# First weight units of the feed-forward layers and of the projection taken token chunk by token chunk

## The chip, the cores and the metric

One Trainium2 chip, one of its cores. The metric is device time in microseconds (us) from the first to the last instruction; lower is better. Engines: PE (TensorE, matrix multiplications), DVE (VectorE), ACT (ScalarE), POOL (GpSimd), SP (SyncE, here a queue that issues DMAs).

## The reference, cut to what matters

One inference step of a two-layer decoder with 1024 prompt tokens and 8 x 4 sample tokens, 1056 token columns in all. Every sub-layer first norms its input; the change sits in the first steps after three of these norms.

```python
h = rmsnorm(x, norm_g[i, 1]) * (1 + sc) + sh          # per token
x = x + gt * swiglu(h, ffn_w_in[i], ffn_w_out[i])     # both layers
def swiglu(h, w_in, w_out):
    g, u = jnp.split(h @ w_in, 2, axis=-1)
    return (jax.nn.silu(g) * u) @ w_out
p = h @ w_in          # layer 1: q, k, v and indexer columns, the projection
```

## The kernel before, in words

Activations lie transposed, features on the 128 partitions (8 feature tiles, KD), tokens along the free axis, in three token chunks of 352 columns (CH, NCH). fp32 products are made of split halves: a value is rounded to a high half (ACT) and the rest is its low half; a product is three matmuls, high-high, low-high and high-low. One result of 128 rows by 352 tokens is a **group** of 8 x 3 = 24 matmuls in one PSUM bank (a feed-forward output tile of the down pass has only 6).

Weights come in units of 1 MB (SP), rounded by ACT (`split_hi`, L623, L814) and their low half made by POOL (`split_lo`, L647, L846; semaphore `w_lo` counts finished units).

The phases run in this order: a front phase with the pooling mixer, feed-forward layer 0 (`ffn_phase`, about 218 to 1018 us of the trace), the projection (`projection_phase`, about 1018 to 1273 us), indexing and attention, the output projection, feed-forward layer 1 (from about 2184 us), the last norm.

**The norm** (`SplitNorm`) works chunk by chunk. ACT squares the 8 tiles of a chunk (L247), the squares are added (L256, L259: chunk 0 on DVE, chunks 1 and 2 on POOL), PE sums over partitions (`pe_sums`, L267), DVE scales (`variance`, L314), ACT takes the root (`act_std`, L281), DVE the reciprocal (`invert`, L319). Then each tile goes through DVE (g, L344), ACT (high half, L291), DVE (low half, L348); `lo_ready` counts finished tiles. Chunk 2 also has the 32 sample columns (`sample`, L326 to L330, and L354). The order of each engine is written out by hand in `act_all`, `dve_all`, `pool_all` and `pe_chunk`. POOL has: adds of chunk 1, split of unit 0, adds of chunk 2, split of unit 1. `pe_chunk(ch)` first makes the sum of chunk ch+1, then waits for the tiles of chunk ch.

**The feed-forward loop** has 11 iterations of three weight units: two hold gate and up columns (a = 0, 1), one the down columns. For each a and chunk PE makes a gate group and an up group; ACT takes silu of the gate (L630), DVE multiplies it with up and splits the product (L716, L718, L720); then the down pass (L696 to L698, 24 output tiles of 6 matmuls) and DVE's residual add (L80). PE has all three chunks of a = 0, then all three of a = 1, then the down pass, which waits for the third unit (L680). In iteration 0 the first pass meets the norm's chunks one by one.

**The projection** has 9 units with two output tiles each (the last has one): for each tile all three chunks. PE takes unit 0 tile by tile, so only one group of each chunk is there to be done while the next chunk is normed. ACT and DVE evict a group in halves (L839, L894), SP writes them out (L796, L797). POOL makes the low half of unit u, then loads 16 pages of indexer keys (`load_index_pages`, L743), and so on for units 2 to 8 (L852 to L854).

Of the kernel before, what the change touches and what calls it, by code (L numbers as in the profile page):

```python
# [16 lines left out]
F32 = mybir.dt.float32  # L17
# [194 lines left out]
class SplitNorm:  # L212
# [80 lines left out]
    def act_all(self, act, split_weights):  # L293
# [12 lines left out]
        split_weights(1)  # L306
        self.act_hi(act, 16, 24)

    def dve_all(self, dve):
# [25 lines left out]
        for ch in range(NCH):  # L335
# [14 lines left out]
            if ch < 2:  # L350
                variance(ch + 1)
                invert(ch + 1)
        dve.wait_ge(self.s_hi, 1)
        dve.tensor_tensor(self.hlo[:, :, SEQ:T], self.hs[:], self.hhi[:, :, SEQ:T].bitcast(F32), ALU.subtract).then_inc(self.s_lo, 1)  # L354
        dve.wait_ge(self.lo_ready, 3 * KD)
        dve.wait_ge(self.s_lo, 1)

    def pool_all(self, pool, split_weights):
        self.add_squares(pool, 1)
        split_weights(0)  # L360
        self.add_squares(pool, 2)
        split_weights(1)
# [212 lines left out]
def ffn_phase(nc, c, d, layer):  # L575
# [3 lines left out]
    with ExitStack() as ctx:  # L579
# [8 lines left out]
        sg, af = norm.sq, norm.g  # L588
        raw_ready = [sem("raw_ready0"), sem("raw_ready1")]
# [8 lines left out]
        def _(sp):  # L598
# [5 lines left out]
            with sp.Fori(0, N - 1) as i:  # L604
                for a in range(3):

                    sp.wait_ge(w_lo, i * 3 + (3, 2, 4)[a])
                    sp.dma_start(raw[:, a % 2, :], src[bass.ds(i * 3 + 3 + a, 1)].rearrange("a p n -> (a p) n")).then_inc(raw_ready[a % 2], 16)

# [4 lines left out]
        def _(act):  # L614
# [40 lines left out]
        def _(pe):  # L655
            norm.pe_sums(pe, 0)

            def iteration(i, first):
                for a in range(2):
                    pe.wait_ge(w_lo, 3 * i + (a + 1))  # L660
                    hi = whi[:, a, :].rearrange("p (k s m) -> p k s m", k=KD, s=2)
                    lo = wlo[:, a, :].rearrange("p (k s m) -> p k s m", k=KD, s=2)
                    for ch in range(NCH):
                        col = slice(ch * CH, (ch + 1) * CH)
                        if a == 0 and first:
                            norm.pe_chunk(pe, ch)
                        for side in range(2):
                            bank = 2 * ch + side
                            if a == 0 and not first:
                                pe.wait_ge(added, i * GD + (bank - 5))  # L670
# [4 lines left out]
                            for k in range(KD):  # L675
                                pe.matmul(c.ps[:, bank, 0:CH], hi[:, k, side, :], hhi[:, k, col], start=(k == 0), stop=False)  # L676
                                pe.matmul(c.ps[:, bank, 0:CH], lo[:, k, side, :], hhi[:, k, col], start=False, stop=False)  # L677
                                last = pe.matmul(c.ps[:, bank, 0:CH], hi[:, k, side, :], hlo[:, k, col], start=False, stop=(k == KD - 1))  # L678
                            last.then_inc(up_ready if side else gate_ready, 1)
# [3 lines left out]
                for ch in range(NCH):  # L683
                    col = slice(ch * CH, (ch + 1) * CH)
                    pe.wait_ge(a_ready, i * 6 + (NCH + ch + 1))
# [19 lines left out]
        def _(dve):  # L705
            norm.dve_all(dve)

            with dve.Fori(0, N) as i:
                for a in range(2):
                    for ch in range(NCH):  # L710
                        q = a * NCH + ch
                        dve.wait_ge(silu_ready, i * 6 + (q + 1))
                        dve.wait_ge(up_ready, i * 6 + (q + 1))
                        s = af[:, q % 2, :]
                        col = slice(ch * CH, (ch + 1) * CH)
                        dve.tensor_tensor(s, sg[:, q % 2, :], c.ps[:, 2 * ch + 1, 0:CH], ALU.mult).then_inc(gated, 1)  # L716
                        dve.wait_ge(gated, i * 6 + (q + 1))
                        dve.tensor_copy(ahi[:, a, col], s).then_inc(a_step, 1)  # L718
                        dve.wait_ge(a_step, i * 6 + (q + 1))
                        dve.tensor_tensor(alo[:, a, col], s, ahi[:, a, col].bitcast(F32), ALU.subtract).then_inc(a_ready, 1)  # L720
                        if q >= 1:
                            dve.wait_ge(a_ready, i * 6 + q)
                for ch in range(NCH):
                    for m in range(KD):
# [4 lines left out]
                        residual_add(dve, c, c.ps[:, q % 6, 0:CH], m, ch, 2 * layer + 1, tmp[:], (rstep, i * KD + (m + 1)), added)  # L729
            dve.wait_ge(added, N * GD)  # L730
# [16 lines left out]
def projection_phase(nc, c, d):  # L747

    NU = 9
    with ExitStack() as ctx:  # L750
# [24 lines left out]
        n_split = [m for m in MS if split_tile(m) is not None]  # L775
        n_f32 = [m for m in MS if f32_dst(m) is not None]
# [3 lines left out]
        def _(sp):  # L780
# [4 lines left out]
            for m in MS:  # L785
                u = m // 2
                if m % 2 == 0 and u + 2 < NU:
                    sp.wait_ge(w_lo, u + 1)
                    sp.dma_start(raw[:, u % 2, :], d.win[u + 2]).then_inc(raw_ready[u % 2], 16)
                for ch in range(NCH):  # L790
                    col = slice(ch * CH, (ch + 1) * CH)
                    sp.wait_ge(act_read, 3 * m + ch + 1)
                    if split_tile(m) is not None:
                        sp.wait_ge(dve_read, 3 * m + ch + 1)
                        q = (3 * n_split.index(m) + ch) % 3
                        sp.dma_start(d.halves[split_tile(m), 0, :, col], shi[:, q, :].bitcast(F32)).then_inc(split_out[q], 16)  # L796
                        sp.dma_start(d.halves[split_tile(m), 1, :, col], slo[:, q, :].bitcast(F32)).then_inc(split_out[q], 16)  # L797
                    if f32_dst(m) is not None:
                        q = (3 * n_f32.index(m) + ch) % 3
                        sp.dma_start(f32_dst(m)[:, col], sf[:, q, :]).then_inc(f32_out[q], 16)  # L800
# [3 lines left out]
            for q in range(3):  # L804
                sp.wait_ge(split_out[q], 32 * len(n_split))
                sp.wait_ge(f32_out[q], 16 * len(n_f32))

        @block.scalar
        def _(act):
            def split_hi(u):  # L810
                act.wait_ge(raw_ready[u % 2], 16 * (u // 2 + 1))
                if u >= 2:
                    act.wait_ge(ready, 6 * (u - 1))
                act.activation(whi[:, u % 2, :], raw[:, u % 2, :], ACT.Copy).then_inc(w_hi, 1)  # L814
            norm.act_all(act, split_hi)
            n = 0
            for m in MS:
                if m % 2 == 0 and m >= 2 and m // 2 + 1 < NU:
                    split_hi(m // 2 + 1)
                for ch in range(NCH):  # L820
                    act.wait_ge(ready, 3 * m + ch + 1)
                    src = c.ps[:, (3 * m + ch) % 6, 0:CH]
                    last = None
                    if f32_dst(m) is not None:
                        k = n_f32.index(m)
                        if k:
                            act.wait_ge(f32_out[ch], 16 * k)
                        last = act.activation(sf[:, ch, :], src, ACT.Copy)
                    if m in samples and ch == 2:
                        last = act.activation(sq[:, samples.index(m), :], src[:, CP2:CH], ACT.Copy)  # L830
                    if split_tile(m) is not None:
                        k = n_split.index(m)
                        if k:
                            act.wait_ge(split_out[ch], 32 * k)
                        if last is not None:
                            last.then_inc(step, 1)
                            n += 1
                            act.wait_ge(step, n)
                        last = act.activation(shi[:, ch, :], src, ACT.Copy)  # L839
                    last.then_inc(act_read, 1)  # L840
# [17 lines left out]
        def _(pe):  # L858
            norm.pe_sums(pe, 0)

            def unit(u, slot, first=False, tiles=2):
                pe.wait_ge(w_lo, u + 1)
                hi = whi[:, slot, :].rearrange("p (k m) -> p k m", k=KD)
                lo = wlo[:, slot, :].rearrange("p (k m) -> p k m", k=KD)
                for m in range(tiles):
                    for ch in range(NCH):
                        q = 3 * m + ch
                        if first and m == 0:
                            norm.pe_chunk(pe, ch)
                        if not first:  # L870
                            pe.wait_ge(act_read, u * 6 + (q - 5))
                            pe.wait_ge(dve_read, u * 6 + (q - 5))
                        col = slice(ch * CH, (ch + 1) * CH)
                        for k in range(KD):
                            w = slice(m * P, (m + 1) * P)
                            pe.matmul(c.ps[:, q, 0:CH], hi[:, k, w], hhi[:, k, col], start=(k == 0), stop=False)  # L876
                            pe.matmul(c.ps[:, q, 0:CH], lo[:, k, w], hhi[:, k, col], start=False, stop=False)
                            last = pe.matmul(c.ps[:, q, 0:CH], hi[:, k, w], hlo[:, k, col], start=False, stop=(k == KD - 1))
# [1033 lines left out]
```

## Time and profile before

| what | value |
|---|---|
| three runs | 3021.97, 3023.41, 3024.28 us; median 3023.41 |
| profiled execution | span 3025.1 us, and no time outside it is shown |
| PE busy | 2520.1 us, 83% of the span |
| DVE, POOL, ACT busy | 48%, 25%, 23% |
| mean granted clock of PE | 0.911 of full speed |

PE is the engine with the most work, so time is won where PE stands still or runs at the lower clock. In the timeline a line has the start in us, the duration in us, the engine, the program line, the operation, what it writes and reads, and in brackets how long its engine was idle before it and what ended that.

### The profile page before, as it was taken

How to read it: one execution, taken by the hardware profiler on the slowest of the kernel's cores; microseconds unless marked ns; L12 is line 12 of the kernel's file. 1: busy time of each engine (PE TensorE's matmuls, PEld its weight loads, DVE VectorE, ACT ScalarE, POOL GpSimd, SP SyncE). 2: the span in 40 equal slices, each digit the busy share in tenths (PEclk: the TensorE clock that was granted, in tenths of full speed). 3: DMA queues.
4: the chain of work that ended last, by engine and by line, in shares of the span. 5: the costliest groups of instructions: out<-in, count | busy, mean ns of one | idle time of the engine just before them, and what ended most of it. 6: DMA issues, size and time to landing. Idle time of an engine off the chain costs nothing. (4 is left out here: it accounts for less than half of the span.)

```text
span 3025.1 us, 40642 instructions
## 1 busy us (share of the span) xinstructions
PE 2520.1 (83%) x14573; PEld 2225.2 (74%) x14573; DVE 1439.8 (48%) x3100; ACT 694.4 (23%) x1162; POOL 744.9 (25%) x557
## 2 busy tenths in 40 slices
PE   7866999999999689784312789697869999999995
PEld 3446999999999589741112567345869999999994
DVE  2747333333333730179997578344273333333336
ACT  2113111111110322150001888312131111111101
POOL 0223121121121235410000677521131211221110
PEclk9887999999999799896655999888979999999997
DMA  9421111111110234552121110571011111111101
GB/s 368 166 94 56 42 42 42 42 42 69 42 42 14 99 113 162 152 121 81 56 69 28 39 32 16 182 268 56 29 56 42 42 42 42 42 64 47 42 14 57
DMA packets 89864, 230.67 MB, mean 76 GB/s; under 512 B 15764, under 2 KB 52724, under 8 KB 73396
## 3 DMA queue, kind: packets, MB, share of 16 engines
q1 hardware_dynamic: 75856, 205.33, 19.6%
q0 software_dynamic: 10400, 22.18, 2.3%
q10 hardware_dynamic: 3524, 2.07, 0.2%
q8 instruction: 49, 0.80, 0.1%
q14 instruction: 35, 0.29, 0.0%
HBM read 200.77 MB, written 28.76 MB: 76 GB/s over the span
## 5 line engine op out<-in xcount | busy, mean ns | idle before, releaser
L676 PE MATMUL ps<-f_hhi,f_whi 128*128 128x352 f32 x2112 | 687.2, 325 | 33.9 <-DVE f_hlo L348 18.4
L677 PE MATMUL ps<-f_hhi,f_wlo 128*128 128x352 f32 x2112 | 681.7, 323 | 0.0
L678 PE MATMUL ps<-f_hlo,f_whi 128*128 128x352 f32 x2112 | 680.9, 322 | 0.0
L647 POOL TENSOR_TENSOR f_wlo<-f_raw,f_whi 128x2048 fp32r<-128x2048 f32 x66 | 304.0, 4607 | 1110.1 <-ACT f_whi L623 1110.1
L80 DVE SCALAR_TENSOR_TENSOR xT<-ps,mod,xT 128x352 f32<-128x352 f32 (+1 forms) x576 | 327.9, 572 | 219.8 <-PE ps L698 121.4
L676 PEld LDWEIGHTS ps<-f_hhi,f_whi 128*128 128x128 f32 x2112 | 400.4, 190 | 37.6 <-DVE f_hlo L348 37.6
L677 PEld LDWEIGHTS ps<-f_hhi,f_wlo 128*128 128x128 f32 x2112 | 401.0, 190 | 0.0
L678 PEld LDWEIGHTS ps<-f_hlo,f_whi 128*128 128x128 f32 x2112 | 400.1, 189 | 0.0
L696 PE MATMUL ps<-f_ahi,f_whi 128*128 128x352 f32 x1056 | 340.6, 323 | 0.0
L697 PE MATMUL ps<-f_ahi,f_wlo 128*128 128x352 f32 x1056 | 338.3, 320 | 0.0
L698 PE MATMUL ps<-f_alo,f_whi 128*128 128x352 f32 x1056 | 338.1, 320 | 0.0
L623 ACT ACTIVATE f_whi<-f_raw 128x2048 fp32r<-128x2048 f32 x66 | 126.4, 1915 | 554.2 <-PE ps L698 418.2
L1396 POOL TENSOR_TENSOR pa_pr<-pa_pr,pa_rl 128x128 f32<-128x128 f32 (+7 forms) x128 | 142.8, 1147 | 368.1 <-DVE pa_rl L1376 368.0
L716 DVE TENSOR_TENSOR f1n_g<-f1n_sq,ps 128x352 f32<-128x352 f32 x66 | 34.4, 521 | 399.4 <-PE ps L678 396.9
L716 DVE TENSOR_TENSOR f0n_g<-f0n_sq,ps 128x352 f32<-128x352 f32 x66 | 34.4, 521 | 398.1 <-PE ps L678 395.7
L697 PEld LDWEIGHTS ps<-f_ahi,f_wlo 128*128 128x128 f32 x1056 | 198.4, 188 | 0.0
L696 PEld LDWEIGHTS ps<-f_ahi,f_whi 128*128 128x128 f32 x1056 | 198.1, 188 | 0.0
L698 PEld LDWEIGHTS ps<-f_alo,f_whi 128*128 128x128 f32 x1056 | 197.9, 187 | 0.0
L876 PE MATMUL ps<-pj_hhi,pj_whi 128*128 128x352 f32 x408 | 135.0, 331 | 19.0 <-DVE pj_hlo L354 11.0
L1067 PE MATMUL ps<-ix_part,rowsum 128*128 128x1 f32 x64 | 16.3, 324 | 156.3 <-DVE ix_rel L1165 156.2
L179 PE MATMUL ps<-ada_raw,silu 128*9 128x256 f32 x576 | 129.2, 388 | 14.5 <-ACT silu L431 14.5
L1316 PE MATMUL ps<-kst,pa_qst 128*128 128x512 f32 (+3 forms) x192 | 75.2, 392 | 73.7 <-DMA pa_qst<-halves 41.7
(307 smaller groups left out, 3939.0 us busy)
## 6 DMA issues: line engine op xcount, KB each, us to landing
f_raw<-in_ffn SPq DMA_DIRECT2D x66, 1024.0 KB, 4.8
ada_raw<-in_ada SPq DMA_DIRECT2D x36, 1024.0 KB, 5.0
sa_kv<-in_ckv POOLq DMA_DIRECT2D x54, 256.0 KB, 4.3
ix_vT<-in_ada SPq DMA_DIRECT2D x12, 1024.0 KB, 4.8
sa_kv<-in_ckv SPq DMA_DIRECT2D x42, 256.0 KB, 4.4
pj_raw<-in_win SPq DMA_DIRECT2D x9, 1024.0 KB, 5.8
pa_qst<-halves SPq DMA_DIRECT2D x128, 64.0 KB, 2.4
halves<-pj_shi SPq DMA_DIRECT2D x45, 176.0 KB, 1.9
```

The costliest lines, as they stand in the source:

```text
L80: ins = dve.scalar_tensor_tensor(out=x, in0=psum[:, 0:n], scalar=gate[:, 0:1], in1=x, op0=ALU.mult, op1=ALU.add)
L179: last = pe.matmul(self.sums(u), self.c.silu[:, k, :], w[:, k, :], start=(k == 0), stop=(k == KD - 1))
L623: act.activation(whi[:, a, :], raw[:, a % 2, :], ACT.Copy).then_inc(w_hi, 1)
L647: pool.tensor_tensor(wlo[:, a, :], raw[:, a % 2, :], whi[:, a, :].bitcast(F32), ALU.subtract).then_inc(w_lo, 1)
L676: pe.matmul(c.ps[:, bank, 0:CH], hi[:, k, side, :], hhi[:, k, col], start=(k == 0), stop=False)
L677: pe.matmul(c.ps[:, bank, 0:CH], lo[:, k, side, :], hhi[:, k, col], start=False, stop=False)
L678: last = pe.matmul(c.ps[:, bank, 0:CH], hi[:, k, side, :], hlo[:, k, col], start=False, stop=(k == KD - 1))
L696: pe.matmul(c.ps[:, q % 6, 0:CH], hi[:, k, w], ahi[:, k, col], start=(k == 0), stop=False)
L697: pe.matmul(c.ps[:, q % 6, 0:CH], lo[:, k, w], ahi[:, k, col], start=False, stop=False)
L698: last = pe.matmul(c.ps[:, q % 6, 0:CH], hi[:, k, w], alo[:, k, col], start=False, stop=(k == 1))
L876: pe.matmul(c.ps[:, q, 0:CH], hi[:, k, w], hhi[:, k, col], start=(k == 0), stop=False)
L1396: pool.tensor_tensor(p, p, rl[:, i % 3, g:g + 1].to_broadcast([P, (q + 1) * P]), ALU.mult).then_inc(p_ready, 1)
```

## The change

In iteration 0 of each feed-forward layer PE takes, for each chunk, the gate and up groups of a = 0 and of a = 1 (four groups) before the next chunk. q = 2 ch + a numbers these pairs. In the projection it takes, for each chunk, the four tiles of units 0 and 1. The second unit is therefore split earlier: on ACT right behind chunk 0's high halves, on POOL ahead of chunk 2's adds. The evictions (silu and gates; high and low halves) of chunk 0 are put on ACT and DVE ahead of chunk 2's norm (`between(0)`), the rest behind the norm (`between(1)`). Iteration 0 is taken out of ACT's and DVE's loops. Core of the diff:

```diff
     def act_all(self, act, split_weights, between):
...
         split_weights(0)
         self.act_hi(act, 0, 8)
+        split_weights(1)
         self.act_std(act, 1)
...
         self.act_std(act, 2)
-        split_weights(1)
+        between(0)
         self.act_hi(act, 16, 24)
+        between(1)
     def dve_all(self, dve, between):
...
             if ch < 2:
                 variance(ch + 1)
                 invert(ch + 1)
+            if ch == 1:
+                between(0)
...
         dve.wait_ge(self.s_lo, 1)
+        between(1)
     def pool_all(self, pool, split_weights):
         self.add_squares(pool, 1)
         split_weights(0)
+        split_weights(1)
         self.add_squares(pool, 2)
-        split_weights(1)
 # ffn_phase
+        FIRST = [(0, 1), (2, 3, 4, 5)]
+            def first_silus(qs):
+                for q in qs:
+                    act.wait_ge(gate_ready, q + 1)
+                    if q >= 2:
+                        act.wait_ge(gated, q - 1)
+                    act.activation(sg_first(q), c.ps[:, 2 * (q % 3), 0:CH], ACT.Silu).then_inc(silu_ready, 1)
-            norm.act_all(act, lambda a: split_hi(a, 0, True))
+            norm.act_all(act, lambda a: split_hi(a, 0, True), lambda half: first_silus(FIRST[half]))
             split_hi(2, 0, True)
-            with act.Fori(0, N - 1) as i:
+            for a in range(3):
+                split_hi(a, 1)
+            with act.Fori(1, N - 1) as i:
+            def first_up():
+                for ch in range(NCH):
+                    norm.pe_chunk(pe, ch)
+                    for a in range(2):
+                        q = 2 * ch + a
+                        if ch == 0:
+                            pe.wait_ge(w_lo, a + 1)
+                        for side in range(2):
+                            if q >= 3:
+                                pe.wait_ge(gated if side else silu_ready, q - 2)
+                            group(a, side, 2 * (q % 3) + side, ch)
+            norm.dve_all(dve, lambda half: first_gates(FIRST[half]))
+            down(0)
+            with dve.Fori(1, N) as i:
 # projection_phase
+        ORDER = [(m, ch) for ch in range(NCH) for m in range(4)] + [(m, ch) for m in range(4, 17) for ch in range(NCH)]
             def split_hi(u):
                 act.wait_ge(raw_ready[u % 2], 16 * (u // 2 + 1))
                 if u >= 2:
-                    act.wait_ge(ready, 6 * (u - 1))
+                    act.wait_ge(ready, 10 if u == 2 else 6 * (u - 1))
+            def evict(n):
+                m, ch = ORDER[n]
+                act.wait_ge(ready, n + 1)
...
+                    if k >= 3:
+                        act.wait_ge(split_out[k % 3], 32 * (k // 3))
...
+            def first_evictions(half):
+                for n in range(0, 4) if half == 0 else range(4, 12):
+                    evict(n)
+            norm.act_all(act, split_hi, first_evictions)
+            for n in range(12, len(ORDER)):
+                m, ch = ORDER[n]
+                if ch == 0 and m % 2 == 0:
+                    if m == 4:
+                        split_hi(2)
+                    if m // 2 + 1 < NU:
+                        split_hi(m // 2 + 1)
+                evict(n)
+            def first_units():
+                for ch in range(NCH):
+                    norm.pe_chunk(pe, ch)
+                    for m in range(4):
+                        n = 4 * ch + m
+                        if ch == 0 and m % 2 == 0:
+                            pe.wait_ge(w_lo, m // 2 + 1)
+                        if n >= 6:
+                            pe.wait_ge(act_read, n - 5)
+                            pe.wait_ge(dve_read, n - 5)
+                        group(m // 2, m % 2, n % 6, ch)
```

DVE's `gate(...)` holds the three instructions of L716 to L720, with a wait for its own last one in q = 0 and 1; `first_gates(qs)` calls it. DVE's `first_low(half)` makes the low halves of groups 0 to 3 and 4 to 11. SP walks ORDER too, and asks for units 2 and 3 at n = 0 and n = 1.

## Rows read from the trace of the kernel before

**Rows 1.** Waits of PE over the span: total us, times, longest us.

```profile
PE ps L676 <- DVE f_hlo L348: 18.4, 4, 5.4
...
PE ps L676 <- DVE f_hlo L354: 15.5, 2, 7.9
```

**Rows 2.** Engines in layer 0's first gate and up passes; PEclk is third from the end.

```profile
242.50:307.40 64.90, 52.87 (x291) 51.77 (x292) 39.90 (x55) 23.02 (x37) 20.90 (x10) 0.88 0.14 50
```

**Rows 3.** Timeline of PE in layer 0: start, duration, operation, idle before.

```profile
242.54 0.66 PE L676 MATMUL ps<-f_hhi,f_whi 128*128 128x352 f32 x1 [5.42 <-DVE f_hlo L348]
...
252.84 0.86 PE L267 MATMUL ps<-f0n_rstd,ones 128*128 128x352 f32 x2
258.06 0.66 PE L676 MATMUL ps<-f_hhi,f_whi 128*128 128x352 f32 x1 [4.36 <-DVE f_hlo L348]
...
275.16 0.63 PE L676 MATMUL ps<-f_hhi,f_whi 128*128 128x352 f32 x1 [7.62 <-DVE f_hlo L354]
...
307.38 0.32 PE L696 MATMUL ps<-f_ahi,f_whi 128*128 128x352 f32 x1
```

**Rows 4.** Timeline of DVE in layer 0: reciprocal, low half, sample columns, gates.

```profile
243.48 2.35 DVE L319 RECIPROCAL f0n_rstd<-f0n_rstd 128x352 f32<-128x352 f32 x1 [0.56 <-ACT f0n_rstd L281]
...
248.31 1.30 DVE L348 SCALAR_TENSOR_TENSOR f_hlo<-f0n_g,mod,f_hhi 128x352 fp32r<-128x352 f32 x1
...
261.39 4.34 DVE L326 TENSOR_TENSOR f0n_hs<-xT,f0n_rstd 128x256 f32<-128x256 f32 x1
...
300.03 0.52 DVE L716 TENSOR_TENSOR f0n_g<-f0n_sq,ps 128x352 f32<-128x352 f32 x1 [6.17 <-PE ps L678]
...
300.96 0.53 DVE L720 TENSOR_TENSOR f_alo<-f0n_g,f_ahi 128x352 fp32r<-128x352 f32 x1
307.65 0.52 DVE L716 TENSOR_TENSOR f0n_g<-f0n_sq,ps 128x352 f32<-128x352 f32 x1 [6.17 <-PE ps L678]
```

**Rows 5.** Timeline of POOL in layer 0: four adds of chunk 2, split of unit 1.

```profile
248.28 4.50 POOL L259 TENSOR_TENSOR f0n_rstd<-f0n_rstd,f0n_sq 128x352 f32<-128x352 f32 x4 [0.29 <-ACT f0n_sq L247]
260.85 4.61 POOL L647 TENSOR_TENSOR f_wlo<-f_raw,f_whi 128x2048 fp32r<-128x2048 f32 x1 [8.06 <-ACT f_whi L623]
```

**Rows 6.** Timeline of ACT in layer 0: weight split, table load, a silu.

```profile
258.88 1.89 ACT L623 ACTIVATE f_whi<-f_raw 128x2048 fp32r<-128x2048 f32 x1
...
275.71 1.28 ACT L630 ACT_TABLE_LOAD   x1
...
288.49 0.47 ACT L630 ACTIVATE f0n_sq<-ps 128x352 f32<-128x352 f32 x1 [1.11 <-PE ps L678]
```

**Rows 7.** Timeline of PE in layer 1 and in the projection.

```profile
2209.22 0.66 PE L676 MATMUL ps<-f_hhi,f_whi 128*128 128x352 f32 x1 [5.42 <-DVE f_hlo L348]
...
2275.33 0.32 PE L696 MATMUL ps<-f_ahi,f_whi 128*128 128x352 f32 x1
...
1043.83 0.66 PE L876 MATMUL ps<-pj_hhi,pj_whi 128*128 128x352 f32 x1 [5.42 <-DVE pj_hlo L348]
...
1076.29 0.63 PE L876 MATMUL ps<-pj_hhi,pj_whi 128*128 128x352 f32 x1 [10.97 <-DVE pj_hlo L354]
```

**Rows 8.** DMA issues of the page: KB each, median us from issue to landing.

```profile
xT<-in_ckidx POOLq DMA_DIRECT2D x128, 32.0 KB, 2.1
...
halves<-pj_slo SPq DMA_DIRECT2D x45, 176.0 KB, 2.4
```

**Rows 9.** Timeline of POOL in the projection: splits of units 2 and 8, last page load.

```profile
1096.58 4.60 POOL L846 TENSOR_TENSOR pj_wlo<-pj_raw,pj_whi 128x2048 fp32r<-128x2048 f32 x1 [30.01 <-ACT pj_whi L814]
...
1236.80 4.62 POOL L846 TENSOR_TENSOR pj_wlo<-pj_raw,pj_whi 128x2048 fp32r<-128x2048 f32 x1
...
1259.29 0.52 POOL L743 DMA_DIRECT2D xT<-in_ckidx  x1 [0.77 <-issue]
```

**Rows 10.** End of the projection: eviction of the last group, next phase's first DMA.

```profile
1265.56 0.46 ACT L828 ACTIVATE pj_sf<-ps 128x352 f32<-128x352 f32 x1 [2.80 <-PE ps L878]
...
1273.04 0.38 SPq L947 DMA_DIRECT2D ix_vT<-o_vT  x1
```

More of the change, by code:

```diff
@@ L588, in ffn_phase @@
         sg, af = norm.sq, norm.g
+        sg0, af0 = sb("sg0", [P, 2, CH]), sb("af0", [P, CH])
         raw_ready = [sem("raw_ready0"), sem("raw_ready1")]
@@ L674, in iteration @@
                                 pe.wait_ge(gated, i * 6 + (ch + 1))
[L675 to L679, printed above, removed]
+                            group(a, side, bank, ch)
                 pe.wait_ge(w_lo, 3 * i + 3)
@@ L705, in _, with gate, down @@
         def _(dve):
[L706 to L722, printed above, removed]
+            def gate(i, q, s, sgq, bank, a, ch, alone=False):
+                dve.wait_ge(silu_ready, i * 6 + (q + 1))
+                dve.wait_ge(up_ready, i * 6 + (q + 1))
+                col = slice(ch * CH, (ch + 1) * CH)
+                dve.tensor_tensor(s, sgq, c.ps[:, bank, 0:CH], ALU.mult).then_inc(gated, 1)
+                dve.wait_ge(gated, i * 6 + (q + 1))
+                dve.tensor_copy(ahi[:, a, col], s).then_inc(a_step, 1)
+                dve.wait_ge(a_step, i * 6 + (q + 1))
+                dve.tensor_tensor(alo[:, a, col], s, ahi[:, a, col].bitcast(F32), ALU.subtract).then_inc(a_ready, 1)
+                if q >= 1:
+                    dve.wait_ge(a_ready, i * 6 + q)
+                if alone:
+                    dve.wait_ge(a_ready, q + 1)
+            def down(i):
                 for ch in range(NCH):
@@ L859, in _, with group, unit @@
             norm.pe_sums(pe, 0)
-            def unit(u, slot, first=False, tiles=2):
-                pe.wait_ge(w_lo, u + 1)
+            def group(slot, m, bank, ch):
                 hi = whi[:, slot, :].rearrange("p (k m) -> p k m", k=KD)
                 lo = wlo[:, slot, :].rearrange("p (k m) -> p k m", k=KD)
+                col = slice(ch * CH, (ch + 1) * CH)
+                for k in range(KD):
+                    w = slice(m * P, (m + 1) * P)
+                    pe.matmul(c.ps[:, bank, 0:CH], hi[:, k, w], hhi[:, k, col], start=(k == 0), stop=False)
+                    pe.matmul(c.ps[:, bank, 0:CH], lo[:, k, w], hhi[:, k, col], start=False, stop=False)
+                    last = pe.matmul(c.ps[:, bank, 0:CH], hi[:, k, w], hlo[:, k, col], start=False, stop=(k == KD - 1))
+                last.then_inc(ready, 1)
+            def first_units():
+                for ch in range(NCH):
+                    norm.pe_chunk(pe, ch)
[7 more added lines that the diff above has]
+                        group(m // 2, m % 2, n % 6, ch)
+            def unit(u, slot, tiles=2):
+                pe.wait_ge(w_lo, u + 1)
                 for m in range(tiles):
@@ L867, in unit @@
                         q = 3 * m + ch
[L868 to L878, printed above, removed]
-                        last.then_inc(ready, 1)
-            unit(0, 0, True)
-            unit(1, 1)
+                        pe.wait_ge(act_read, u * 6 + (q - 5))
+                        pe.wait_ge(dve_read, u * 6 + (q - 5))
+                        group(slot, m, q, ch)
+            first_units()
             with pe.Fori(1, 4) as i:
```

143 lines of the change are left out of this document (78 added, 65 removed).

## The prediction

> **What bounds the kernel now.** I read the waits of PE first, then the stretch of a first iteration, then the timelines of each engine there. In the waits [rows 1] the reader is to see that PE, the busiest engine, stands still for the norm: it waits for the low halves of a chunk (four times over both layers) and for the sample columns (twice). The stretch [rows 2] is layer 0 from its first gate matmul to its down pass: 64.9 us of which PE is busy 52.9, at a mean granted clock of 0.88. The timeline [rows 3] shows where: chunk 0 starts at 242.54, chunk 1 at 258.06 (4.36 us idle, and the 0.86 us sum just before), chunk 2 at 275.16 (7.62 us idle), the down pass at 307.38. After each wait the first matmul takes 0.63 to 0.66 us instead of 0.32: PE is back at the lower of its two levels, 1.2 GHz. Two figures follow. Warm, 48 matmuls take 7.63 us (gates at 300.03 and 307.65 [rows 4]), 0.159 us each. Chunk 0's pair took 252.84 - 242.54 - 0.16 = 10.14 us, so a cold start costs 2.5 us.
>
> **The work of PE is only moved.** No matmul is added or removed. Before, eight groups of 24 are left when chunk 2 is ready; afterwards four. That is the gain, 4 x 3.82 = 15.3 us, if chunk 2 is not later and nothing new waits. Both happen, so I follow the chains in layer 0.
>
> **Chunk 1.** ACT now splits unit 1 right after chunk 0's high halves, which end about 1 us before PE starts, at 241.6 (an estimate). So 1.89 us [rows 6] until 243.5, then POOL 4.6 us [rows 5] until 248.2. ACT's root of chunk 1 stands behind the split and comes 0.5 us later; the reciprocal, 2.35 us even while POOL adds [rows 4], ends at 246.3. Then DVE needs two SBUF operands, and such an instruction does not run while POOL splits: the sample product took 4.34 us [rows 4] because the split of unit 1 ran from 260.85 to 265.46 [rows 5]. So DVE stands until 248.2. POOL's seven adds of chunk 2 start only then, and ACT's square 19, which needs the first add, holds up the high halves queued behind it until 249.6; DVE's first three tiles cover that. While POOL adds, a DVE low half takes 1.30 us [rows 4] beside adds of 1.13 us [rows 5]. All seven adds now fall on DVE work, where before some fell on the reciprocal. Walked tile by tile with these prices, chunk 1 is ready at 260.8, 2.7 us later than before.
>
> Meanwhile PE has 96 matmuls of chunk 0: 242.54 + 10.14 + 7.63 = 260.3, the second unit being there since 248.2. Then comes the sum of chunk 2, 0.86 us, until 261.2. The late chunk is covered by 0.4 us; without cover, each us late counts. PE does chunk 1's 96 matmuls warm until 276.5.
>
> **Chunk 2.** Its scaling on DVE waits for that sum, which now stands behind chunk 0's four groups. From the sum it takes as long to the end of the reciprocal as from chunk 1's end to the sample product, 258.06 to 261.39, about 3.5 with the hop from PE: 264.7. ACT loads the silu table (1.28) and makes two silus (0.47 each) [rows 6] beside that reciprocal; even a load back would lie in ACT's wait for the sample columns. Then the two gates put ahead of the sample columns cost DVE 2 x (300.96 + 0.53 - 300.03 = 1.46) = 2.9 [rows 4]: 267.7. From the sample product's start to PE's chunk 2 it was 261.39 to 275.16, 13.8 us, of which the split took 4.34 less some 0.4 (estimate, from 0.53 for 352 columns). That split is gone from here: 9.85 us remain, chunk 2 at 277.6. PE idles 1.1 us. For the clock no row shows a wait this short here; bounds are 0 and 2.5, and I take 0. PE's four groups end at 277.6 + 15.25 = 292.85.
>
> **A new wait: the third unit.** ACT's split of the down weights now stands behind silu q = 5, which needs the last gate group at 277.6 + 11.45 = 289.05. Then 0.47 + 1.89 + 4.6 and the hops: 296.1. Before, it was ready long ahead. PE idles 3.2 us and starts cold (2.5; bounds 0 and 2.5; I take 2.5, as the 4.36 us wait is nearest). The down pass counts from 298.6 instead of 307.38: **8.8 us won**. DVE's last gate conversion is held up by the same split; its operands are needed only in the down pass's last third. SP's next load also waits for the third unit, 16 us later than before, but PE wants it 24 x 6 x 0.159 = 22.9 us after the down pass starts, and behind the two splits (6.5 us) 16 us are left for the load. So no loss.
>
> Layer 1 shows the same steps shifted by 2209.22 - 242.54 = 1966.7 [rows 7]: down pass at 2265.3 instead of 2275.33, **10.0 us**.
>
> **The projection**, shifted by 801.3 [rows 7]: sum of chunk 2 done at 1062.5, reciprocal 1066.0. Ahead of the sample columns stand four low halves; the fourth eviction reuses slot 0 and so waits until SP has written group 0 out: 0.53 for its low half, SP's two issues 0.4, 2.4 us to landing [rows 8], then 0.46 + 0.53. That ends at 1070.5 where low halves alone would end at 1068; chunk 2 at 1080.3 against 1076.29. SP asks for unit 3's megabyte ahead of group 1's output, but that slot is needed only at 1079. PE has idled 2.5 us; cold, its four groups end at 1098.1. Now the last eviction (0.7), ACT's split of unit 2, which stands behind it (1.89), and POOL's (4.6): PE waits 7.3 us, until 1105.4, and starts cold. POOL's split of unit 2 starts at 1100.8 instead of 1096.58 [rows 9], 4.2 later. From there POOL is the bound: splits and page loads run back to back, 140.2 us from the split of unit 2 to that of unit 8 [rows 9], while PE needs 6 x 22.9 = 137.3. So the low half of unit 8 is ready at 1245.6, PE ends at 1257.1 instead of 1265.5, the last page load lands at 1259.29 + 4.2 + 2.1 = 1265.6 [rows 8, 9]. Before, the next phase began 7.5 us after PE's end [rows 10]; from PE that would be 1264.6, so POOL's loads decide: about 1266 against 1273.04, **7.0 us**.
>
> **Sum.** 8.8 + 10.0 + 7.0 = 25.8 us. On the profiled execution's 3025.1 that is 2999.3; this execution is 1.7 us above the median of 3023.4, so the forecast is 2997.6. Its own range: with no cold starts behind the new waits 7.5 more (2990); with cold starts at chunk 2 in both layers and a landing 3 us later, 8 less (3005.6).
>
> **Rivals.** (a) Nothing new waits. Then the layers win 307.38 - 292.85 = 14.5 each, and the projection's PE runs on from 1098.1 over 39 groups of 3.815 to 1246.9, 18.6 us earlier: 2975.8. Against it stand ACT's order and POOL's back-to-back chain.
>
> (b) DVE and POOL share nothing in chunk 1. Then an add and a low half take turns, 1.13 + 0.57 = 1.7 us instead of 1.3, seven times: chunk 1 is 2.8 later, 2.4 of it uncovered, 7 us in three places: 3004.8. If the split holds the reciprocal up too, it is 2.35 more each: 3011.9. For it speaks the 4.34 us stall, against it the 1.30 us row and the reciprocal's 2.35. The Trainium skill, page SBUF — State Buffer, section Who interferes with whom, says that of a VectorE instruction with two SBUF inputs and a GpSimd one that reads SBUF the later is blocked until the first has finished; by that rule the first time of (b) would come out, while the row shows partial overlap, and the measurement decides.
>
> (c) The change does not do what it says: unit 1's low half comes no earlier than its 265.5. PE then waits 12.6 us inside chunk 0 and nearly all of the gain is gone: about 3020. Against it: only ACT's place in the order held that split back.
>
> (d) Slower. The new wait of 3.2 us before the down pass leaves PE at the lower level through the whole pass: 144 x 0.159 = 22.9 us per layer, and the 7.3 us wait does so to unit 2, 22.9 again: 68.7 less the 25.8: 3066. It turns the sign once 25.8 / 0.159 = 162 matmuls more run at half speed. Against it: 48 matmuls behind a 5.42 us wait lost only 2.5 us.
>
> **How the numbers follow.** The forecast 0.75, (a) 0.06, (b) 0.12, (c) 0.04, (d) 0.03. The range reaches from 2988 to 3008: it takes in the forecast's bounds and the first half of (b), and leaves out (a), (c), (d), the end of (b) and tails. Within 0.2% (6 us, about what a measurement of this kernel can tell from no change) lie (c) and a bit of (b): 0.05. Slower: 0.03. Faster: 0.92.
>
> **What would show it.** Right: no PE idle between chunk 0 and chunk 1, about 1 us ahead of chunk 2 in the layers and 2.5 in the projection, 3 us of idle put down to POOL's split ahead of the first down matmul, 7 us ahead of unit 2, and the next phase after the projection waiting for page loads. Wrong: an idle time ahead of chunk 1 (b), PE at the lower level long into the down pass (d), or no idle ahead of it (a).

## The result and the profile after

The changed kernel takes 3010.57 us (median of four runs, 3007.39 to 3013.15) against 3023.85 for the kernel before; the ratio is 0.9948, with an interval of 0.9934 to 0.9961. That is 11.8 to 20.0 us faster, where 25.8 were forecast. The profiled execution is the fastest of the four, 3007.39 us; its span is 3005.6.

What answers to [rows 1], the waits of PE (total us, times, longest), in the kernel after:

```profile
PE ps L1121 <- DMA ix_kiwi<-kiwi: 26.7, 1, 26.7
PE ps L686 <- DVE f_hlo L350: 21.7, 4, 10.2
...
PE ps L927 <- DVE pj_hlo L350: 12.3, 2, 10.2
```

The two entries of [rows 1] (18.4 and 15.5 us, six waits) have become one of 21.7 us in four waits. Two of these are the wait of 10.2 us ahead of chunk 0; the waits ahead of chunk 1 are gone. (The wait ahead of chunk 0 was 5.42 us before, because PE made the sum of chunk 1 later then, behind unit 0's low half; from the layer's first square to its first gate matmul it is 24.6 us in both kernels.) The new first line belongs to the phase behind the projection, and is the clue to what follows. Before, it was:

```profile
PE ps L1044 <- DMA ix_kiwi<-kiwi: 14.8, 1, 14.8
```

The stretch that answers to [rows 2], from layer 0's first gate matmul to its down pass, after (us, busy time of PE, PEld, DVE, ACT, POOL, then the granted clock third from the end):

```profile
243.96:297.50 53.54, 49.67 (x290) 48.56 (x290) 39.65 (x57) 19.74 (x36) 16.58 (x9) 0.95 0.00 1
```

64.9 us have become 53.5, and PE's clock there is 0.95 instead of 0.88. The timeline of PE after (start, duration, operation, idle before), in the order of layer 0, the projection, layer 1, answers to [rows 3, 7]:

```profile
243.96 0.66 PE L686 MATMUL ps<-f_hhi,f_whi 128*128 128x352 f32 x1 [10.16 <-DVE f_hlo L350]
278.88 0.40 PE L686 MATMUL ps<-f_hhi,f_whi 128*128 128x352 f32 x1 [0.65 <-DVE f_hlo L350]
297.54 0.66 PE L734 MATMUL ps<-f_ahi,f_whi 128*128 128x352 f32 x1 [3.16 <-POOL f_wlo L670]
298.00 0.49 PE L735 MATMUL ps<-f_ahi,f_wlo 128*128 128x352 f32 x1
...
1035.72 0.66 PE L927 MATMUL ps<-pj_hhi,pj_whi 128*128 128x352 f32 x1 [10.16 <-DVE pj_hlo L350]
1072.14 0.40 PE L927 MATMUL ps<-pj_hhi,pj_whi 128*128 128x352 f32 x1 [2.14 <-DVE pj_hlo L350]
1095.23 0.63 PE L927 MATMUL ps<-pj_hhi,pj_whi 128*128 128x352 f32 x1 [7.50 <-POOL pj_wlo L906]
...
2199.98 0.66 PE L686 MATMUL ps<-f_hhi,f_whi 128*128 128x352 f32 x1 [10.15 <-DVE f_hlo L350]
2234.82 0.40 PE L686 MATMUL ps<-f_hhi,f_whi 128*128 128x352 f32 x1 [0.70 <-DVE f_hlo L350]
2253.50 0.66 PE L734 MATMUL ps<-f_ahi,f_whi 128*128 128x352 f32 x1 [3.16 <-POOL f_wlo L670]
```

Every wait that the prediction placed is there, nearly in the size it gave. Yet the sum is missed. To see where, I cut both executions at the same events. A layer runs from chunk 0's first gate matmul to the first square of the next norm; the projection from its first square to the next phase's first DMA. Layers begin at 242.54 and 2209.22 [rows 3, 7] before, at 243.96 and 2199.98 after. For the kernel before, the first squares of the norms behind the layers lie at 1018.64 and 2986.58, for the kernel after at 1010.54 and 2966.84; the next phase's first DMA lies at 1273.04 [rows 10] and 1266.34:

| stage, us | before | after | won | forecast |
|---|---|---|---|---|
| layer 0 | 776.1 | 766.6 | 9.5 | 8.8 |
| layer 1 | 777.4 | 766.9 | 10.5 | 10.0 |
| projection | 254.4 | 255.8 | -1.4 | 7.0 |

The rest of the 19.5 us between the spans is 0.9 us in phases with the same code. So the layers gave what was forecast and the projection gave nothing, although PE ends earlier in it. The three stages give 18.6 us, which lies within the interval of the ratio. POOL, ACT and SP in the projection after, answering to [rows 9, 10]:

```profile
1090.49 4.50 POOL L906 TENSOR_TENSOR pj_wlo<-pj_raw,pj_whi 128x2048 fp32r<-128x2048 f32 x1 [40.91 <-ACT pj_whi L863]
...
1230.48 4.63 POOL L906 TENSOR_TENSOR pj_wlo<-pj_raw,pj_whi 128x2048 fp32r<-128x2048 f32 x1
...
1246.93 0.46 ACT L875 ACTIVATE pj_sf<-ps 128x352 f32<-128x352 f32 x1 [2.80 <-PE ps L929]
...
1253.55 0.52 POOL L792 DMA_DIRECT2D xT<-in_ckidx  x1 [0.85 <-issue]
...
1266.34 0.38 SPq L1024 DMA_DIRECT2D ix_vT<-o_vT  x1
```

PE's last group is evicted 236.4 us after the phase's first square, against 246.9 before [rows 10]; SP's next DMA, 7.5 us behind it before, now comes 19.4 us behind it. What ended the projection? In the profile each engine's part of a phase, its block, ends with an instruction called DRAIN, and the EVENT_SEMAPHOREs of all engines come together behind the last of these. The projection's last ones in the kernel before (engine's queue, operation, duration in ns, first and last start in us):

```profile
L750 POOLq DRAIN  x1: 9283/9283/9283, 1261.5 to 1261.5; - x1
...
L750 SPq DRAIN  x1: 7/7/7, 1271.7 to 1271.7; - x1
```

And in the kernel after:

```profile
L799 SPq DRAIN  x1: 7/7/7, 1253.4 to 1253.4; - x1
...
L799 POOLq DRAIN  x1: 9283/9283/9283, 1255.7 to 1255.7; - x1
L799 SPq EVENT_SEMAPHORE  x1: 17/17/17, 1265.1 to 1265.1; - x1
```

POOL ends its block with a DRAIN of 9.28 us. Before, it lay from 1261.5 to 1270.8, and SP, which waits for its last write, was done at 1271.7: the DRAIN was covered by 0.9 us and no wait pointed to it. After, SP is done at 1253.4 and then stands still until 1265.1. Measured from the phase's first square, SP's end moved from 253.1 to 242.9, but POOL's from 252.1 to 254.4, and the later of the two counts. PE's first work of the next phase waits 26.7 us instead of 14.8 for a transfer that SP can't issue sooner. POOL is later since its chain starts later: the split of unit 2 comes 79.95 us after the first square instead of 77.94, and to the split of unit 8 it is 139.99 us, against 140.22 before [rows 9]: the chain is back to back in both kernels.

### The profile page after: what moved, and what is told of

It is laid out like the page before. It is cut to its first block and busy times, and to the rows that moved or that the text cites. A ratio compares the mean times of both kernels' runs of the same rounds, so it can differ in the third digit from the quotient of the medians.

```text
span 3005.6 us, 40525 instructions
## 1 busy us (share of the span) xinstructions
PE 2511.4 (84%) x14573; PEld 2217.1 (74%) x14573; DVE 1435.8 (48%) x3100; ACT 670.1 (22%) x1144; POOL 744.0 (25%) x557
## 5 line engine op out<-in xcount | busy, mean ns | idle before, releaser
L686 PE MATMUL ps<-f_hhi,f_whi 128*128 128x352 f32 x2112 | 683.9, 324 | 21.9 <-DVE f_hlo L350 21.7
L927 PE MATMUL ps<-pj_hhi,pj_whi 128*128 128x352 f32 x408 | 134.1, 329 | 20.1 <-DVE pj_hlo L350 12.3
L1393 PE MATMUL ps<-kst,pa_qst 128*128 128x512 f32 (+3 forms) x192 | 75.2, 391 | 73.9 <-DMA pa_qst<-halves 41.6
```

Of the source, the lines that this page charges most:

```text
L927: pe.matmul(c.ps[:, bank, 0:CH], hi[:, k, w], hhi[:, k, col], start=(k == 0), stop=False)
```

## Experiments

The theory: POOL's chain of splits, page loads and DRAIN sets the projection's end. Rivals: PE's waits and clock, SP's writes, or a gain that is there and lost elsewhere. The ratios below are to the kernel before, of 4 to 11 executions each, and their intervals reach some 3 to 5 us to either side; the stages of the profiled executions are the finer measure. In stages whose code is the changed kernel's they spread from 765.3 to 768.2 us (layers) and from 255.0 to 257.7 us (projection).

| kernel | won, us (ratio, interval) | layer 0 | layer 1 | projection |
|---|---|---|---|---|
| layers only | 19.1 (0.9937, 0.9923 to 0.9950) | 767.8 | 765.3 | 255.0 |
| projection only | -1.8 (1.0006, 0.9997 to 1.0015) | 776.1 | 776.6 | 257.4 |
| pages ahead | 29.1 (0.9904, 0.9889 to 0.9919) | 768.1 | 768.2 | 248.3 |
| unit 2 early | 23.9 (0.9921, 0.9907 to 0.9936) | 766.3 | 765.7 | 249.3 |
| half of the loads | one execution, no ratio | 766.3 | 765.6 | 245.6 |
| down unit early | 18.5 (0.9939, 0.9926 to 0.9953) | 766.6 | 767.2 | 255.0 |
| three edits | 23.9 (0.9921, 0.9907 to 0.9934) | 766.7 | 767.2 | 249.3 |
| half a group ahead | 33.9 (0.9888, 0.9870 to 0.9906) | 766.4 | 767.5 | 238.9 |
| down unit early, wait | 28.4 (0.9906, 0.9891 to 0.9920) | 762.1 | 762.8 | 257.7 |
| half a group, wait | 43.6 (0.9856, 0.9841 to 0.9871) | 761.5 | 762.4 | 238.8 |

**Layers only.** The projection goes back to its old order, with the old norm class:

```diff
 # projection_phase
-        norm = SplitNorm(nc, ctx, "pjn", c, 2, hhi, hlo)
+        norm = SplitNormBefore(nc, ctx, "pjn", c, 2, hhi, hlo)
```

> The two feed-forward layers as changed, the projection as it was before. Theory (the end of the projection is set by POOL: its last page load, then a DRAIN of 9.28 us, so that the gain of PE there is lost): the layers' gains as read from the two traces remain, 9.6 + 10.6 = 20.2 us, and the 1.4 us that the projection's phase grew by are not paid. Faster than before by about 20 us, faster than the changed kernel by about 1.4 us, and the projection's phase, from its first square to the next phase's first DMA, takes 254.4 us again. Rival (the layers won less than the traces of single executions say, and the projection did win its 7.0): faster than before by only 8 to 13 us, slower than the changed kernel by 7.

Measured: 19.1 us faster than before, the projection 255.0 us. The layers alone give the whole gain.

**Projection only.** The other half:

```diff
 # ffn_phase
-        norm = SplitNorm(nc, ctx, f"f{layer}n", c, 2 * layer + 1, hhi, hlo)
+        norm = SplitNormBefore(nc, ctx, f"f{layer}n", c, 2 * layer + 1, hhi, hlo)
```

> The projection as changed, the two layers as they were before. Theory (POOL's last load and its DRAIN of 9.28 us set the end): no gain, 0 to 1.5 us slower than before; PE's last group is evicted some 20 us before the next phase's first DMA, POOL's DRAIN begins about 245 us after the phase's first square, and SP waits about 12 us at the block's end. Rival (my prediction's step: the end is the landing of the last load, and what was lost went elsewhere in the program): faster than before by 7 us.

Measured: 1.8 us slower, with an interval that reaches from 0.9 faster to 4.5 slower; 7 us faster lies well outside it. SP was done at 1263.9, POOL's DRAIN of 9283 ns began at 1266.1, which is 246.7 us after the first square. The two halves add up: 19.1 - 1.8 = 17.3 against 15.7 for both.

**Pages ahead.** A group of 16 loads goes ahead of the split of unit 2:

```diff
 # projection_phase, gpsimd
+            load_index_pages(pool, c, d, 0, page_ready)
             for u in range(2, NU):
                 split_lo(u)
-                load_index_pages(pool, c, d, u - 2, page_ready)
+                if u < NU - 1:
+                    load_index_pages(pool, c, d, u - 1, page_ready)
```

> The changed kernel, with POOL's first 16 page loads moved ahead of its split of unit 2 (the stretch in which POOL waits for that unit), so that nothing but the DRAIN follows its split of unit 8. PE's work and all waits of PE stay. Theory (POOL's chain with the DRAIN sets the end): POOL's DRAIN ends near 1245 us on the changed kernel's scale instead of 1265.0, then SP's last landing at 1253.4 decides, and the next phase begins near 1254.7 instead of 1266.3: 11.6 us less than the changed kernel, about 25 to 27 less than before. First rival (PE's chain sets the end: cold starts and the 7.5 us wait for unit 2): 0 us against the changed kernel. Second rival (the end is the last landing, not the DRAIN): a DRAIN of 9.28 us that now ends behind SP changes nothing by itself, and the gain is only that of the landing, 1255.7 - 1253.4 = 2.3 us.

Measured: a phase of 248.3 us, 7.5 less than after. The block's end in this kernel:

```profile
L799 POOLq DRAIN  x1: 12293/12293/12293, 1236.2 to 1236.2; - x1
...
L799 SPq DRAIN  x1: 7/7/7, 1257.3 to 1257.3; - x1
```

And POOL's last load and last split there:

```profile
1233.98 0.52 POOL L792 DMA_DIRECT2D xT<-in_ckidx  x1 [0.77 <-issue]
1234.51 4.63 POOL L906 TENSOR_TENSOR pj_wlo<-pj_raw,pj_whi 128x2048 fp32r<-128x2048 f32 x1
```

POOL is done at 1236.2 + 12.3 = 1248.5, and now SP's 1257.3 decides, as the theory said. The DRAIN is longer since it began while the last split ran (1234.51 to 1239.14); from that split's end it is 9.32 us, though the last load had been issued 5.2 us before that end and had landed. So the DRAIN does not wait for a recent load to land. Only 7.5 of 11.6 us came because the 16 loads did not fit in ahead of the split: it began 84.7 us after the first square, 4.8 later than after, PE waited 12.6 us for unit 2, and SP's end came 4.1 us later than after. PE's idle time grew and the phase got shorter, which rules out the rival of PE's waits; the second rival's 2.3 us are too little.

**Unit 2 early.** ACT makes unit 2's high half before the last two evictions:

```diff
 # projection_phase, first_evictions
                     evict(n)
+                    if n == 9:
+                        split_hi(2)
...
-                    if m == 4:
-                        split_hi(2)
```

> The changed kernel, with ACT's high half of unit 2 placed right behind the eviction of the tenth group instead of behind the twelfth (its condition, that PE is done with unit 0, is met there). Theory (POOL's back-to-back chain from the split of unit 2 sets the end): POOL's split of unit 2, the page loads and the DRAIN all come about 7.6 us earlier, PE's wait of 7.5 us ahead of unit 2 is gone, and the next phase begins about 7.6 us earlier: 7 to 8 us less than the changed kernel. Rival (the end of the phase depends on neither POOL nor PE, but on SP's queue of writes): under 1 us.

Measured: a phase of 249.3 us, 6.5 less than after; POOL's split of unit 2 came at 73.9 us instead of 79.95, and PE's wait of 7.5 us is gone. The DRAIN began at 1247.7, SP was done at 1245.5: POOL still ends last, by 2.2 + 9.3 us. Together with the kernel above this leaves POOL's chain alone as the bound: there PE waited longer and POOL ended earlier, here both came earlier, and each time the phase followed the later of POOL and SP.

**Half of the loads.** This kernel leaves out half of the page loads behind each split. `load_index_pages` gets two more arguments for it, how many pages of a group it loads and how many it skips:

```diff
 # projection_phase, gpsimd
-                load_index_pages(pool, c, d, u - 2, page_ready)
+                load_index_pages(pool, c, d, u - 2, page_ready, PAGES // 4)
...
```

> The changed kernel with 8 instead of 16 page loads behind each of POOL's splits in the projection (half of the indexer keys are not loaded, so their scores are left to what lies in the buffer). Theory (the length of POOL's DRAIN grows with the loads that POOL issued in the block: 9.28 us for 113, 2.38 us for 17 and 5.65 us for 63 in other blocks): a DRAIN of 4.6 to 5.3 us for 57 loads. Rival (a fixed length at this place): 9.28 us again. As POOL then has some 9 us of slack in each unit, the splits no longer run back to back, PE and SP's last landing set the end, and the phase is about 12 us shorter than the changed kernel's 255.8 us.

Its block's end:

```profile
L799 POOLq DRAIN  x1: 4710/4710/4710, 1226.3 to 1226.3; - x1
L799 SPq DRAIN  x1: 7/7/7, 1250.5 to 1250.5; - x1
```

57 DMAs of POOL in the block, 4.71 us; 113, 9.28 us. The difference is 4.573 us for 56 loads, 82 ns each. The phase is 10.2 us shorter (12 expected), and SP's last landing sets its end, 19.4 us behind POOL's.

**Down unit early.** This goes at the two waits of 3.16 us in the layers:

```diff
 # ffn_phase, scalar
             def first_silus(qs):
+                if qs[0] == 2:
+                    split_hi(2, 0, True)
                 for q in qs:
...
-            split_hi(2, 0, True)
```

> The changed kernel, with ACT's high half of the down unit placed ahead of the silus of q = 2 to 5 in the layers' first iteration instead of behind them. Theory (in both layers the down pass waits 3.16 us for POOL's low half of that unit, and then starts at the lower level for about 9 matmuls, some 1.3 us): both go, 4.5 us per layer, about 9 us less than the changed kernel; the down pass begins without an idle time put down to POOL's split. Rival (the 1.89 us that ACT then spends ahead of the silus delays the gate groups that need them, and gives the gain back): 0 to 3 us less than the changed kernel, with a new wait of PE for ACT's silu.

Measured: nothing, 766.6 and 767.2 us; but neither theory nor rival is what the trace shows. PE, DVE and POOL in layer 0:

```profile
292.01 9.23 POOL L671 TENSOR_TENSOR f_wlo<-f_raw,f_whi 128x2048 fp32r<-128x2048 f32 x2 [8.79 <-ACT f_whi L637]
...
293.28 0.32 PE L735 MATMUL ps<-f_ahi,f_whi 128*128 128x352 f32 x1
...
294.14 2.70 DVE L751 CAST f_ahi<-f0n_g 128x352 fp32r<-128x352 f32 x1
296.87 4.76 DVE L753 TENSOR_TENSOR f_alo<-f0n_g,f_ahi 128x352 fp32r<-128x352 f32 x1
...
302.18 0.43 PE L735 MATMUL ps<-f_ahi,f_whi 128*128 128x352 f32 x1 [3.01 <-DVE xT L80]
```

The down pass does begin without a wait, at full speed. But ACT now gets to the second iteration's units earlier, POOL splits them from 292.01 on, and DVE's last gate product, in the same microseconds, is held: its cast ends at 296.84, just after the first split (halfway through the 9.23 us, at 296.6), and its low half at 301.63, just after the second (301.24). The residual adds stand behind them, PE's banks stay full, and PE waits 3.01 us. One wait went and another of its size came.

**Down unit early, with a wait.** If that is so, keeping POOL's splits behind the gate product must free the 3 us:

```diff
 # ffn_phase, scalar, on top of the edit above
+            act.wait_ge(a_ready, 6)
             for a in range(3):
                 split_hi(a, 1)
```

> The changed kernel with the down unit's high half ahead of the silus, as before, and a wait of ACT for the last gate product (six low halves of the activations) ahead of its splits of the second iteration's units. Without that wait the down pass began at 293.28 at full speed and then stood still for 3.01 us for DVE's residual add. Theory (POOL's splits of the second iteration, 9.23 us from 292.01, held DVE's cast and low half of the last gate product: 2.70 and 4.76 us instead of 0.34 and 0.53): with the wait those two take 0.34 and 0.53 us, POOL's splits begin behind them and lie beside residual adds of 0.58 us as in the changed kernel, the 3.01 us are gone, and each layer is 4.5 us shorter (766.5 and 766.8 become about 762): 9 us less than the changed kernel. Rival (the residual adds, not the gate product, are what POOL's splits hold up, or the iteration after it starts late for its units): the wait moves and the layers stay within 1.5 us of 766.5.

Measured: layers of 762.1 and 762.8 us, 4.5 and 4.0 less than after. DVE and POOL in layer 0:

```profile
296.42 0.34 DVE L752 CAST f_ahi<-f0n_g 128x352 fp32r<-128x352 f32 x1
296.80 0.53 DVE L754 TENSOR_TENSOR f_alo<-f0n_g,f_ahi 128x352 fp32r<-128x352 f32 x1
...
299.35 9.19 POOL L672 TENSOR_TENSOR f_wlo<-f_raw,f_whi 128x2048 fp32r<-128x2048 f32 x2 [14.08 <-ACT f_whi L637]
299.63 0.58 DVE L80 SCALAR_TENSOR_TENSOR xT<-ps,mod,xT 128x352 f32<-128x352 f32 x1 [0.38 <-PE ps L738]
```

A wait added on ACT made the kernel faster. Beside the same splits a residual add, which reads one operand from PSUM, takes its usual 0.58 us.

**Three edits, and half a group ahead.** Pages ahead, unit 2 early and down unit early in one kernel:

> The changed kernel with three edits together: the down unit's high half ahead of the silus in the layers, unit 2's high half behind the tenth eviction, and the first 16 page loads ahead of POOL's split of unit 2. Theory: the layers give 9 us (if that edit does what is expected of it alone); in the projection the loads ahead of the split keep POOL until about 85 us after the phase's first square, as with that edit alone, so that the earlier high half of unit 2 brings nothing: the phase takes 248 us as with the loads ahead alone, 7.5 less than the changed kernel; together about 16.5 us less than the changed kernel. Rival (the gains of the two projection edits add): the phase takes 241 us, together about 24 us less.

Measured: 249.3 us for the projection, nothing from the layers, where PE again waits 3.01 us for the residual add; that is some 8 us less than the changed kernel by the ratios, and 16.5 were expected. The 16 loads hold POOL until 85.1 us after the first square, so unit 2's earlier high half brings nothing; the gains don't add. Then only 8 loads ahead, which fit into POOL's wait:

```diff
 # projection_phase, gpsimd, on top of the three edits
-            load_index_pages(pool, c, d, 0, page_ready)
+            load_index_pages(pool, c, d, 0, page_ready, PAGES // 4)
             for u in range(2, NU):
                 split_lo(u)
+                load_index_pages(pool, c, d, u - 2, page_ready, PAGES // 4, PAGES // 4)
                 if u < NU - 1:
-                    load_index_pages(pool, c, d, u - 1, page_ready)
+                    load_index_pages(pool, c, d, u - 1, page_ready, PAGES // 4)
```

> As the kernel with all three edits, but only 8 page loads go ahead of the split of unit 2 (they fit into the 10.8 us that POOL waits between chunk 2's last low half and unit 2's high half), and every later group of 16 loads is shifted by 8, so that 8 follow the split of unit 8. Theory: the split of unit 2 begins 74 us after the phase's first square as with the earlier high half alone, the DRAIN begins 8 loads (9.3 us) earlier than there and ends near 238 us, SP's last landing near 236.5 us; the next phase begins about 239 us after the first square instead of 255.8: 17 us from the projection and 9 from the layers, about 26 us less than the changed kernel. Rival (seven more loop starts on POOL cost as much as the loads moved): the phase takes 245 us or more.

Measured: 238.9 us for the projection, 16.9 less than after, as the theory gave. The 9 us expected of the layers are missing (766.4 and 767.5, with the 3.01 us wait in both), so that the whole is some 18 us less than the changed kernel by the ratios instead of 26. The block's end:

```profile
L800 POOLq DRAIN  x1: 9283/9283/9283, 1237.4 to 1237.4; - x1
...
L800 SPq DRAIN  x1: 7/7/7, 1246.8 to 1246.8; - x1
```

POOL (1237.4 + 9.3 = 1246.7) and SP end together. With the wait of ACT added this is the best kernel:

> The kernel with half a group of loads ahead, unit 2's earlier high half and the down unit's earlier high half, plus that wait of ACT in both layers. Theory: the projection keeps its 238.9 us from first square to next phase, and each layer gives 4.5 us: about 9 us less than without the wait, some 26 less than the changed kernel, about 42 less than before. Rival (the layers give nothing, as without the wait): 33 less than before.

Measured: 2983.85 us (median of four, 2979.05 to 2985.69), 43.6 us faster than before by the ratio (41.6 by the medians) where 42 were expected, with the projection at 238.8 and the layers at 761.5 and 762.4.

## Why the prediction was wrong

**The layers were right.** Chunk 1 is covered: in neither layer of the kernel after does idle time stand ahead of it (other kernels with this code show up to 0.7 us there, and up to 1.3 in the projection). Chunk 2 finds PE idle for 0.65 and 0.70 us (1.1 forecast) and its first matmul takes 0.40 us, at a granted clock of 1.00 over the 3 us behind it, so the choice of no cold start holds. The down pass waits 3.16 us for POOL's split (3.2 forecast). Its cold start was put too high: the granted clock is 0.50 from 297.54 to 300.5 and 1.00 behind that, and ten matmuls take 3.04 us where ten at 0.159 take 1.59, which costs about 1.45 us and not 2.5. That, less the smaller things, makes 9.5 and 10.5 of 8.8 and 10.0.

**The projection's inner steps were right too.** ACT waits 4.92 us for the write of a low half before its fourth eviction; chunk 2 starts 36.4 us after chunk 0 (36.5 forecast), after an idle time of 2.14 (2.5); unit 2 is waited for 7.50 us (7.3). The first matmul of chunk 2 took 0.40 us where I had put a cold start, so POOL's split of unit 2 came 2.0 us later than before and not 4.2.

**The step that failed** is the end of the projection: "the last page load lands at 1259.29 + 4.2 + 2.1 = 1265.6", "so POOL's loads decide: about 1266 against 1273.04". I had named POOL as the bound, and ended its chain at a landing. The chain goes on with the DRAIN of 9.28 us, a term that the sum put at nothing. It was in the trace of before, as an instruction of POOL's queue that counts as no busy time and that nothing waited for. With it, my own steps give a DRAIN from 1261.5 + 4.2 = 1265.7 to 1275.0 and, with the 1.3 us that lie between DRAIN and next DMA after (1265.0 to 1266.34), 1276.3: 3.3 us lost instead of 7.0 won. The sum would have been 15.5, the forecast 3007.9; measured is 3010.57. That 15.5 meets the ratio's 15.7 so well is luck in part, for the stages give 20.0 in the layers (18.8 forecast) and -1.4 in the projection (-3.3 by these steps). Nor is it settled that the projection lost anything: with the changed kernel's code it took from 255.0 to 257.7 us in four kernels, with the old code 254.4 and 255.0. Shown by: projection only (no gain), pages ahead and half a group ahead (the gain comes once loads are moved away from the end).

**The rivals.** (a) is out: the new waits are there. (b) is out: chunk 1 was not waited for, so that its second time, 3011.9, lies 1.3 us from the measured one by chance. (c) is out: the second unit was there when PE came to it. (d) is out: the clock rose over the stretch, from 0.88 to 0.95, and was back at 1.00 3 us into the down pass. None of them was the cause; the missing rival was "POOL's block ends later than its last load".

What no run settles: why the median won 15.7 us by its ratio where the two halves add to 17.3; the difference is smaller than the intervals. Nor does any run show why POOL's DRAIN takes time for each DMA.

## What to carry to other kernels

When an engine is named as the next bound, follow its queue to the barrier at the end of the phase, including instructions that count as no work; an engine that ends 0.9 us ahead of another is the bound as soon as the other is sped up. POOL pays for the DMAs of a block again in its DRAIN, however early in the block they were issued, so count that in when its chain is added up, and place them where it waits anyway, in portions that fit. A unit prepared earlier lets the next preparation start earlier too, and what that collides with must be asked: a wait in front of it can win time.

## What the runs showed of the hardware

POOL's DRAIN at the end of a block grew with the DMAs that it had issued there: 4.71 us for 57, 9.28 us for 113, and it was no shorter when the last of them lay further back. The kernel's other blocks show the same price, once the DRAIN is counted from the end of POOL's last work, as in pages ahead. Three of them in the kernel before, and the work that two of these DRAINs begin beside:

```profile
L579 POOLq DRAIN  x2: 4567/4570/4572, 950.5 to 2918.4; - x2
L372 POOLq DRAIN  x1: 2379/2379/2379, 206.9 to 206.9; - x1
L903 POOLq DRAIN  x1: 2849/2849/2849, 1348.0 to 1348.0; - x1
950.40 4.60 POOL L647 TENSOR_TENSOR f_wlo<-f_raw,f_whi 128x2048 fp32r<-128x2048 f32 x1 [18.21 <-ACT f_whi L623]
205.35 2.42 POOL L460 TENSOR_TENSOR pool_dlo<-pool_df,pool_dhi 128x1056 fp32r<-128x1056 f32 x1
```

Layer 0's block has no DMA of POOL, and only 0.07 us of its DRAIN lie behind the split that is still running. In the front phase's block with 17 DMAs 1.47 us lie behind the last work, in the one with 30 it is 2.54 us, although the last of the 30 was issued 46 us earlier, and in the one with 63 (5.65 us, L1448) 5.23. With 57 and 113 all six lie within 0.03 us of 0.07 us and 0.0815 us for each DMA.

While POOL ran its split, both operands in SBUF, DVE's cast (one operand) took 2.70 us instead of 0.34 and its low half (two operands) 4.76 instead of 0.53, each ending within 0.4 us of the split. A residual add with one operand in PSUM kept its 0.58 us. The Trainium skill, page SBUF — State Buffer, section Who interferes with whom, states that a VectorE instruction with two SBUF inputs contends with a GpSimd one that reads SBUF, that a copy or cast in a two-port mode contends with GpSimd too, that whichever was issued first holds the other off for its whole length, and that a VectorE one with at most one SBUF input outside those modes does not contend. The three rows agree, the cast if it ran in such a mode, which no row shows. The 1.30 us of a low half beside an add [rows 4, 5] is less than the 1.70 that whole instructions in turns would give, so in that case the overlap was partial.

An idle time of PE of 0.56 to 2.14 us ahead of chunk 2 left its first matmul at 0.40 us in all these kernels. For longer waits the rows differ: after 2.30 us it was 0.63 in the kernel with half of the loads, after 2.46 us 0.40 in the one with the down unit early. After 3.16 us it was 0.66 in the changed kernel's layer 0, with a granted clock of 0.50 for the next 3 us, and 0.43 in layer 1 of the kernel with half of the loads, with a clock of 1.00. So the length of the wait alone does not decide, and no run shows what does.
